# First attention of a two-block network: stacked queries and keys, transposed outputs, GpSimd scaling the weights

## What is computed

```python
h = rms_norm(x, norm_gain)
(q_n, kc, vc, ks, vs, kw, vw, gate_logits, z_n,
 q_d, k_d, v_d, qi, ki, wi, z_d) = split_columns(h @ w_in, IN_WIDTHS)
# 8 query heads on 2 key/value heads, 64 wide, twice
o_nsa = g[0] * compressed(q_n, kc, vc) + g[1] * selected(q_n, ks, vs) + g[2] * window(q_n, kw, vw)
o_dsa = attention over the 128 keys of highest index score (q_d, k_d, v_d)
mixed = concatenate([o_nsa * silu(z_n), o_dsa * silu(z_d)])
return x + mixed @ w_out
```

## Time and profile before

| | before |
|---|---|
| median of 3 runs | 1795.41 us (1794.2 to 1796.72) |
| the profiled execution, time | 1794.89 us |
| the profiled execution, span | 1793.1 us |
| TensorE busy, mean granted clock | 1735.9 us (97%), 0.99 |
| VectorE, ScalarE, GpSimd busy | 990.4, 741.1, 694.3 us |
| units' first score to last output | 199.3 to 363.0 us |
| output tiles | 371.1 to 425.3 us |

### The profile page before, as it was taken

One profiled execution on the slowest core, in us unless ns is written; L12 is line 12 of the kernel. 1 busy time (PEld: TensorE's weight loads), 2 busy tenths in 40 slices (PEclk: granted clock), 3 DMA queues, 4 the chain that ended last, 5 costly groups with the idle time before them and its releaser, 6 DMA issues. The chain is left out here.

```text
span 1793.1 us, 23296 instructions
## 1 busy us (share of the span) xinstructions
PE 1735.9 (97%) x8345; PEld 1416.5 (79%) x8345; DVE 990.4 (55%) x1657; ACT 741.1 (41%) x1282; POOL 694.3 (39%) x301
## 2 busy tenths in 40 slices
PE   7999998988999999999999999999999999999997
PEld 7777787777888777788888888887777888888886
DVE  5999776474579688633333335789775731111112
ACT  6434555523375564322222223466465343122321
POOL 3424111235430234555445557440211644444442
PEclk9999999999999999999999999999999999999998
DMA  7234010053332224455555532332310323232311
GB/s 251 82 106 141 24 36 25 24 194 121 109 101 100 83 83 149 146 193 192 189 193 194 188 141 94 108 103 84 106 37 24 106 94 100 90 104 94 99 54 47
DMA packets 56633, 197.65 MB, mean 110 GB/s; under 512 B 6993, under 2 KB 8017, under 8 KB 56530
## 3 DMA queue, kind: packets, MB, share of 16 engines
q1 hardware_dynamic: 55666, 194.15, 31.6%
q10 hardware_dynamic: 864, 2.11, 0.3%
HBM read 194.14 MB, written 2.10 MB: 109 GB/s over the span
## 5 line engine op out<-in xcount | busy, mean ns | idle before, releaser
L516 POOL TENSOR_TENSOR WL<-RAW,WH 128x1024 fp32r<-128x1024 f32 x234 | 593.9, 2543 | 872.6 <-ACT WH L600 535.9
L1917 PE MATMUL bank<-HH,WH 128*128 128x512 f32 x1120 | 439.0, 392 | 9.1 <-POOLq L521 5.4
L1919 PE MATMUL bank<-HH,WL 128*128 128x512 f32 x1120 | 437.7, 391 | 0.0
L1918 PE MATMUL bank<-HL,WH 128*128 128x512 f32 x1120 | 437.7, 391 | 0.0
L600 ACT ACTIVATE WH<-RAW 128x1024 fp32r<-128x1024 f32 x259 | 270.6, 1051 | 246.0 <-PE bank L1919 220.0
L1917 PEld LDWEIGHTS bank<-HH,WH 128*128 128x128 f32 x1120 | 211.5, 189 | 54.7 <-issue 8.0
L1919 PEld LDWEIGHTS bank<-HH,WL 128*128 128x128 f32 x1120 | 211.4, 189 | 44.1
L1918 PEld LDWEIGHTS bank<-HL,WH 128*128 128x128 f32 x1120 | 211.4, 189 | 43.6
L1837 DVE TENSOR_TENSOR HF<-SILU,bank 128x512 f32<-128x512 f32 x43 | 29.6, 688 | 301.6 <-PE bank L1919 300.6
L1917 PE MATMUL bank<-HDH,WH 128*128 128x512 f32 x352 | 137.1, 390 | 0.0
L1919 PE MATMUL bank<-HDH,WL 128*128 128x512 f32 x352 | 137.0, 389 | 0.0
(11 more groups left out here) (371 smaller groups left out, 2933.5 us busy)
## 6 DMA issues: line engine op xcount, KB each, us to landing
RAW<-in_stream SPq DMA_DIRECT2D x363, 512.0 KB, 3.3
out_t<-YA SPq DMA_DIRECT2D x8, 256.0 KB, 2.2
X<-in_xt ACTq DMA_DIRECT2D x3, 512.0 KB, 10.8
RAW<-in_stream SPq DMA_DIRECT2D x2, 256.0 KB, 3.9
X<-in_xt ACTq DMA_DIRECT2D x2, 256.0 KB, 6.0
ACC<-in_pos SPq DMA_DIRECT2D x1, 256.0 KB
gains<-in_gains SPq DMA_DIRECT2D x1, 224.0 KB
CS<-in_cs SPq DMA_DIRECT2D x1, 128.0 KB
```

The lines of the kernel that those rows point to most:

```text
L516: nc.gpsimd.tensor_tensor(lo(k)[:], raw(k)[:], hi(k)[:].bitcast(F32), ALU.subtract).then_inc(sem["passed"], mark("passed", *k))
L1917: nc.tensor.matmul(out, A[0], B[0], start=first, stop=False)
L1918: nc.tensor.matmul(out, A[0], B[1], start=False, stop=False)
L1919: return nc.tensor.matmul(out, A[1], B[0], start=False, stop=last)
```

## The change

- **Stacks.** A query head is stored as 128 rows: 64 rounded (high) and 64 of what the rounding left (low), in HH and HL, which are free in this stage. A key is stored as its high part twice (WH) and its low part twice (WL), in the slots of split weights. Scores are then two rounded products, of 128 rows each, instead of one float32 product. ScalarE makes the high parts from the bank (one copy of 64x512 for a query, two for a key), VectorE the low ones (one or two subtractions). Key and query of the first head are stacked ahead of the units; five key stacks, seven query stacks and the short key follow behind units 0 to 13, the eight query stacks of branch 2 behind units 38, 39, 44, 45, 50, 51, 56 and 57 (CONVERT).
- **Order of the units.** By head, both causal branches of a head one after the other, four query tiles each; then branch 2 by head. The lags become 6 (turn) and 8 (product), the weights' ring 8.
- **Scaling.** VectorE takes a reciprocal per unit; GpSimd multiplies the weights by it and by the gate, before they are turned. It also scales the first eight modulation rows, which ScalarE did.
- **Moves.** ScalarE moves turned weights; from unit 28 on VectorE moves those of the two short query tiles.
- **Outputs** are transposed: values with zeros beside them (VZ) are stationary, four products of 512, 384, 256 and 128 columns per head and branch. Two heads and all branches gather in one bank; the compressed branch adds a product of 512 columns per pair. The gate values Z are turned one chunk every sixth unit from 14, VectorE multiplies the bank by them, and high and low parts follow inside the units. The mixture is not turned any more.
- **Elsewhere.** The compressed tiles start at units 15 to 27, the selection rounds stand at every fourth unit from 28 to 60. Output tiles 0 and 1 run partly inside the last units. Among the output tiles the 16 modulation rows stand as 0, 0, 4, 4, 4, 4 where they stood as 2, 3, 3, 3, 3, 2.

```diff
-        order += [ada.pop(0) for _ in range((2, 3, 3, 3, 3, 2, 0, 0)[n])]
+        order += [ada.pop(0) for _ in range((0, 0, 4, 4, 4, 4, 0, 0)[n])]
...
-UNITS1 = [(b, j, g, qt) for b in (0, 1) for j in range(4) for qt in range(NT) for g in range(2)]
-UNITS1 += [(2, j, g, qt) for qt in range(NT) for j in range(4) for g in range(2)]
+UNITS1 = [(b, h % 4, h // 4, qt) for h in range(HEADS) for b in (0, 1) for qt in range(NT)]
+UNITS1 += [(2, h % 4, h // 4, qt) for h in range(HEADS) for qt in range(NT)]
+NSA_UNITS = 2 * HEADS * NT
+RING1, T_LAG1, O_LAG1 = 8, 6, 8
...
+def mover(v):
+
+    return "read_dve" if v >= 28 and v % NT < 2 else "read_act"
...
+MIX_HI = {66: 0, 69: 1, 72: 2, 83: 3, 85: 4, 89: 5, 97: 6}
+MIX_LO_POOL = {70: 0, 73: 1, 77: 2, 86: 3, 89: 4, 92: 5}
+MIX_LO_DVE = {98: 6}
+O1_PASS = (76, 82)
+O1_PARTS = {101: ((0, 0, 3),), 102: ((0, 3, 5),), 103: ((0, 5, 7), (1, 0, 7), (0, 7, 8), (1, 7, 8))}
+
+GATE_TURN = {14 + 6 * c: c for c in range(KD)}
+
+
+TURNS = {5: ("tqn", 1), 8: ("tqn", 2), 11: ("tqn", 3), 13: ("tkc",)}
+TURNS.update({38 + 6 * j: ("tqd", j) for j in range(4)})
+CONVERT = {0: (("tk", 0, 1),), 1: (("tqn", 0, 1),), 2: (("tk", 1, 0),), 3: (("tk", 1, 1), ("tk", 2, 0)),
+           4: (("tk", 2, 1),), 13: (("tkc",),)}
+CONVERT.update({5 + 3 * (j - 1) + g: (("tqn", j, g),) for j in range(1, 4) for g in range(2)})
+CONVERT.update({38 + 6 * j + g: (("tqd", j, g),) for j in range(4) for g in range(2)})
...
+O1_SPLITS = (75, 80, 101)
+
+
+CMP_START = (15, 19, 23, 27)
...
-TOPK_UNITS = tuple(range(2, 56, 6))
+TOPK_UNITS = tuple(range(28, 64, 4))
...
+        VZ = w("VZ", [P, NT, 13 * DH], F32, 24)
...
+        PT1 = (at("PT1a", [P, NT, S], F32, (split0 + 16) * KB), w("PT1b", [P, NT, S], F32, 8))
```

On GpSimd, for every unit:

```diff
+            for v in range(len(UNITS1)):
+                br, j, g, qt = UNITS1[v]
+                n = (qt + 1) * P
+                pool.wait_ge(sem["p_inv"], value("p_inv", v))
+                p_, over = PR[v % RING1][:, 0:n], COEF1[:, v % 16:v % 16 + 1]
+                if br == 2:
+                    ins = nc.gpsimd.tensor_scalar(p_, p_, over, ones[:, 0:1], ALU.mult, ALU.mult)
+                else:
+                    col = 3 * (4 * g + j) + 1 + br
+                    ins = nc.gpsimd.tensor_scalar(p_, p_, over, gate[:, qt, col:col + 1], ALU.mult, ALU.mult)
+                ins.then_inc(sem["p_pool"], mark("p_pool", v))
+                if v - 1 in ATT_ADA:
+                    pass_to(SLOT[("ada", 0, ATT_ADA.index(v - 1))] + 1)
```

On ScalarE, the high parts, and their place behind the exponential of a unit:

```diff
+                act.wait_ge(sem["full"], value("full", kind, i))
+                b = bank_of(kind, i)[rows_of(g), :]
+                if kind == "tk":
+                    k_hi, _ = key_stack(i, g)
+                    nc.scalar.activation(k_hi[rows_of(1 - g), :], b, ACT.Copy)
+                    ins = nc.scalar.activation(k_hi[rows_of(g), :], b, ACT.Copy)
+                else:
+                    ins = nc.scalar.activation(query_stack(kind, 4 * g + i)[rows_of(g), :], b, ACT.Copy)
+                ins.then_inc(sem["stack_hi"], mark("stack_hi", kind, i, g))
+
...
+                for x in CONVERT.get(u, ()):
+                    stack(*x)
```

On VectorE, the low parts, the outputs of a pair, and what stands in the unit loop:

```diff
+            def stack_low(kind, *at_):
+
+                dve.wait_ge(sem["stack_hi"], value("stack_hi", kind, *at_))
...
+                if kind == "tk":
+                    k_hi, k_lo = key_stack(i, g)
+                    for r in range(2):
+                        ins = V.tensor_tensor(k_lo[rows_of(r), :], b, k_hi[rows_of(g), :].bitcast(F32), ALU.subtract)
...
+                    q = query_stack(kind, 4 * g + i)
+                    ins = V.tensor_tensor(q[rows_of(1 - g), :], b, q[rows_of(g), :].bitcast(F32), ALU.subtract)
...
+            def mix_pair_out(c):
+
+                dve.wait_ge(sem["read_act"], value("read_act", "tz", c))
+                dve.wait_ge(sem["full"], value("full", "oc", c))
+                V.tensor_tensor(gated(c), bank_of("oc", c)[:].rearrange("p (t q) -> p t q", t=NT), gated(c),
+                                ALU.mult).then_inc(
+                    sem["read_dve"], mark("read_dve", "oc", c))
...
+                v = u - 1
+                if 0 <= v < nU:
+                    dve.wait_ge(sem["read_act"], value("read_act", "s", 1, v))
+                    V.reciprocal(COEF1[:, v % 16:v % 16 + 1], RSUM1[:, v % 16:v % 16 + 1]).then_inc(
+                        sem["p_inv"], mark("p_inv", v))
+                v = u - T_LAG1
+                if 0 <= v < nU and mover(v) == "read_dve":
...
+                for x in CONVERT.get(u, ()):
+                    stack_low(*x)
```

On TensorE, in the unit loop:

```diff
-                    nc.tensor.matmul(b[:, 0:n], (QNT if br < 2 else QDT)[:, j, qt * P:(qt + 1) * P],
-                                     KT[:, 2 * br + g, 0:n], start=True, stop=False)
+                    for i, part in enumerate(key_stack(br, g)):
+                        nc.tensor.matmul(b[:, 0:n], query_stack(kind, 4 * g + j)[:, qt * P:(qt + 1) * P],
+                                         part[:, 0:n], start=(i == 0), stop=False)
...
-                    for kb in range(qt + 1):
-                        c = br * P + g * DH
-                        last = nc.tensor.matmul(b, PT1[:, v % RING, kb * P:(kb + 1) * P],
-                                                G[4][:, kb, c:c + DH], start=(kb == 0), stop=(kb == qt))
...
+                    m = 2 * (2 * br + g) + 1 - j % 2
+                    for kb in range(NT):
+                        last = nc.tensor.matmul(
+                            pair_bank[c][:, kb * P:S], VZ[:, kb, DH * m:DH * m + P], PT1[e % 2][:, kb, kb * P:S],
+                            start=(kb == 0 and NT * e == first),
+                            stop=(kb == NT - 1 and c >= 4 and NT * e + NT - 1 == end))
```

More of the change, by code:

```diff
@@ L227 @@
 RING = 4
-def evictor(v):
-    return "read_dve" if v % 4 == 3 else "read_act"
 UNITS2 = [(h, qt) for h in range(HEADS) for qt in range(NT)]
@@ L2127, in _ @@
             pe.wait_ge(sem["read_act"], value("read_act", "p1", 4, 3))
-            turn(("tc", 1), [G[4][:, tt, 384:512] for tt in range(NT)])
+            turn(("tc", 1), [VC[:, tt, :] for tt in range(NT)])
             project(3)
```

375 lines of the change are left out of this document (211 added, 164 removed).

## The result

| | before | after |
|---|---|---|
| median | 1796.07 us (4 runs, 1794.2 to 1796.93) | 1829.21 us (4 runs, 1826.17 to 1831.36) |
| ratio | | 1.0186, 95% interval 1.017 to 1.0201 |
| profiled execution: time, span | 1794.89, 1793.1 us | 1831.15, 1829.3 us |
| TensorE busy, mean granted clock | 1735.9 us, 0.99 | 1732.5 us, 0.974 |

The change makes the kernel slower by 1.9%, some 33 us. I had forecast 1792.5 us, with 1780 to 1804 as the range. TensorE has no more work than before; it waits more and runs at its lower clock more.

The account below looks back on a forecast made before the run. TensorE was taken to set the pace before the change; its gains would be paid back by chains through VectorE and ScalarE in units 0 to 63. Seven stages summed to 2.8 us less, 1792.5 us, range 1780 to 1804.

Parts of the forecast that it names:

- Units 0 to 13: Units 0 to 13: maximum, exponential, copies and subtractions go in turn, neither engine ahead; sum 38 us.
- Units 14 to 27: Units 14 to 27: TensorE sets the pace with 26 us of work, plus 1 for a fallen clock.
- Units 38 to 63: Units 38 to 63: VectorE's work of 38 us plus waits sets the pace, 46 us where TensorE has 36.
- in four the score that follows has to wait for the bank of the query: Units 38 to 63: in four units the next score waits for the bank holding the query, 2.4 us in all.
- Unit 64 to the last output: Unit 64 to the last output: units 64 to 95, then last turns, outputs and tile 0's first blocks; 53.5 us.
- My fourth case: Units 64 to 95: scaling costs its upper end, GpSimd becomes the bound, some 5 us; forecast time 1797 us, chance 0.10.
- Tiles: Last output to tile 7: VectorE's 16 modulation rows (27 us), additions, a split, then tiles 6 and 7; 46.5 us.
- The fast one: Units 0 to 13 and 28 to 63: copies or subtractions shorter, or TensorE's pace holds in 38 to 63; 1782 us, chance 0.27.
- the port: Units 38 to 63: GpSimd's scaling and VectorE hold each other's port, 10 us; forecast time 1802 us, chance 0.18.
- unit 28 about 25 us later than before: Sign of being right: unit 28 starts about 25 us later than its earlier 237.5.
- VectorE near 90% busy: Sign of being right: VectorE near 90% busy in units 38 to 63.
- The first stretch's slow clock lasting far past unit 14: Sign of being wrong: TensorE's slow clock from units 0 to 13 continues far past unit 14.

Follow-up runs that it names:

- e1: Kernel after the change, but in units 0 to 13 ScalarE makes a unit's high parts before that unit's exponential, not behind it; 1815.06 us, ratio 1.0115.
- e11: Kernel after with e1, e2, earlier gate copies, e7's later turn, spread modulation rows, and both query heads stacked together in units 5, 8, 11; 1785.93 us.
- e2: Kernel after the change, but both heads sharing a turned query of branch 2 are stacked in one unit (38, 44, 50, 56); 1815.02 us, ratio 1.0106.
- e7: Kernel after with e1 and e2, and the eight modulation rows from GpSimd turned by TensorE at unit 75 instead of 71; 1795.26 us, ratio 0.9996.

## Why the prediction was wrong, step by step

- **First score.** 198.1 forecast, 198.35 measured.
- **Units 0 to 13** (5.7 us too low). The mechanism was right, and e1 shows it. A query stack's unit takes 2.25 us from maximum to maximum (219.05 to 221.30), where my terms for it give 0.42 + 0.47 + 1.4 = 2.3, and the four units with key stacks take 17.5 us, where I had 17.3 (4.0 + 12.2 + 1.1). The mis-sized term is TensorE's scores: VectorE waited 4.7 us for them in five places, where I put 1.0 for first score and bank, and took 1.5 off for the two units without a stack, which waited 0.8 and 1.0. The reciprocals, which I left out, cost next to nothing here: most stand where VectorE waits for ScalarE anyway (219.51, then 0.91 us idle).
- **Units 14 to 27** (7.8 too low). The step that sums TensorE's work to 26 had it right: with the gate copy's wait gone these units took 28.0 us at a clock of 1.00 (e11), 1.5 of it in three short waits. It took a bank as free that ScalarE frees a unit late, and put 1 us for a clock that has fallen. The waits are 3.1 us, and behind each come 3 to 5 us at the lower clock (259 to 262.5, 271.5 to 276).
- **Units 38 to 63** (13.4 too low): **the step that failed.** That VectorE has 46 us here "where TensorE has 36" did not decide (its 38 us of work measured 33.9), and the term "in four the score that follows has to wait for the bank of the query", put at 2.4 us, was the real bound. I had the place and even the order rows that show it, but priced the delay of one maximum on VectorE. The price is TensorE's standstill, from its last allowed product until the second head is taken: 15.4 us in four waits, and a clock of 0.83 behind them. e2 takes away 14.5 of it in the stretch. That e2's 44.9 is near my 46 is chance: VectorE is not the bound in either.
- **Unit 64 to the last output** (7.4 too low). The work was right, 53.5 against 54.4 in e7. What was missing is one wait of 3.9 us for GpSimd's eighth row. My fourth case ("GpSimd becomes the bound of units 64 to 95") had the engine and the size, some 5 us, but not the mechanism: it was 39.6 us busy of 60.9.
- **Tiles** (4.3 too low). The path, VectorE's rows and then tiles 6 and 7, was the right one; its rows ended 34.3 us behind the last output, where I had 32, though they cost less than my 27 (14 of 1.53 us and 2 of 0.75). TensorE waited 2.3 and 2.4 us for splits behind two of the groups of four rows, and from the split of tile 6 (448.8) to tile 7 it took 13.9 us, where I had 11.7, at a clock of 0.81 and 0.85 in the ten microseconds from 447 on. I had counted the rows as a sum and not where they lie.
- **The rivals.** The fast one (VectorE's and ScalarE's work in the first and fourth stage shorter) and the port: both refuted. I gave 0.26 to slower, and my slow cases all were an engine or a port that becomes full. None was an in-order engine standing still in front of a bank.
- **The signs.** "unit 28 about 25 us later than before" (237.5 before): 39.2 later. "VectorE near 90% busy" in units 38 to 63: 33.85 of 59.39, 57%. "TensorE under 85%" there came true (73%), by its waits. "The first stretch's slow clock lasting far past unit 14" was a sign of being wrong; the clock of units 14 to 27 was indeed 0.85, but it stood at 1.00 from 241 to 257 and fell anew behind the waits for the gate copy.

In these stretches 40.0 us lie between forecast and measurement. e1 and e2 take away 29.1, and the gate copy, the modulation and the rows up to 7, 6 and 4 more: 46 in all, more than 40, since e1 also shortens the chain that I had forecast. How much of each gain is the wait and how much the clock behind it is not settled: no run changes the clock alone where TensorE sets the pace.
